# A chunked delta-rule stage on one core: right sides in turn with the last level's products, and GpSimd's streams behind VectorE's

## The reference

```python
def wkv_scan(r, w, k, v, kk, a, s0, reverse):
    def step(s, inp):
        r_t, w_t, k_t, v_t, kk_t, a_t = inp
        sa = jnp.einsum('bhij,bhj->bhi', s, -kk_t)
        s = (s * w_t[:, :, None, :] + sa[..., None] * (kk_t * a_t)[:, :, None, :]
             + v_t[..., None] * k_t[:, :, None, :])
        return s, jnp.einsum('bhij,bhj->bhi', s, r_t)
    ...

def rwkv_mix(streams, s0, ln_w, ln_b, r_k, g_up):
    r, v, kk, per_dir, gd = streams
    (wf, kf, af), (wb, kb, ab) = per_dir
    yf, sf = wkv_scan(r, wf, kf, v, kk, af, s0[0], False)
    yb, sb = wkv_scan(r, wb, kb, v, kk, ab, s0[1], True)
    y = yf + yb
    ...
    return y.reshape(b, l, D_RWKV) * g, (sf, sb)
```

## Time and profile before

| | us |
|---|---|
| median of 3 runs | 3325.36 |
| lowest and highest | 3323.35 and 3326.42 |
| the profiled execution's own time | 3319.18 |
| its span | 3317.4 |
| TensorE busy | 3078.1 (93%) |
| VectorE busy | 1578.4 (48%) |
| ScalarE busy | 564.4 (17%) |
| GpSimd busy | 1234.7 (37%) |

### The profile page before, as it was taken

How to read it: one execution, slowest core, us unless ns; L and a number is a source line. 1 busy time by engine, 2 the same in 40 slices (tenths; PEclk the granted TensorE clock), 3 DMA queues, 4 the chain that set the end, 5 groups by cost and what they waited for, 6 DMA issues and landing times.

```text
span 3317.4 us, 69293 instructions
## 1 busy us (share of the span) xinstructions
PE 3078.1 (93%) x32062; PEld 2768.7 (83%) x32062; DVE 1578.4 (48%) x2216; ACT 564.4 (17%) x1042; POOL 1234.7 (37%) x725
## 2 busy tenths in 40 slices
PE   4998998998999999999998788897999999999998
PEld 4877887877887888788698677777989999999998
DVE  4655276446337720378842677776344441113111
ACT  1022202011120120200002445453010000000001
POOL 2000010000000001134274454443648887777774
PEclk7998999998999999999999999999999999999999
DMA  7964288666226634367842000000546554444442
GB/s 269 420 242 181 103 315 317 269 263 241 104 100 241 259 126 183 127 249 297 310 160 91 6 6 9 6 6 26 193 151 233 222 208 169 162 178 147 162 176 101
DMA packets 55921, 583.08 MB, mean 176 GB/s; under 512 B 7202, under 2 KB 9568, under 8 KB 10704
## 3 DMA queue, kind: packets, MB, share of 16 engines
q1 hardware_dynamic: 38080, 466.11, 37.4%
q0 software_dynamic: 17552, 112.54, 8.9%
HBM read 576.52 MB, written 2.10 MB: 174 GB/s over the span
## 4 chain that ended last, share of the span: by engine, by line
PE 70%; DVE 14%; DMA 9%; issue 3%; POOL 2%; ACT 1%; SPq 0%; ACTq 0%; DVEq 0%; POOLq 0%
PE PS L1712 23%; PE PS L374 15%; PE PS L672 7%; PE PS L1665 5%; DMA ring<-in_w_vec_dram 4%; DMA ring<-in_w_second_dram 2%; PE PS L1891 2%; DVE ring L2304 2%; PE PS L417 2%; DMA ring<-in_w_start_dram 1%; PE PS L371 1%; PE PS L1908 1%; PE PS L1906 1%; PE PS L1837 1%; PE PS L1729 1%
## 5 line engine op out<-in xcount | busy, mean ns | idle before, releaser
L374 PE MATMUL PS<-H,ring 128*128 128x256 f32 x2944 | 668.8, 386 | 7.0 <-ACT H L702 7.0
L374 PEld LDWEIGHTS PS<-H,ring 128*128 128x128 f32 x2944 | 562.1, 193 | 94.9 <-issue 17.6
L1712 PE MATMUL PS<-H,ring 128*128 128x128 f32 x3424 | 403.9, 275 | 2.4 <-DMA ring<-in_w_second_dram 2.4
L1712 PEld LDWEIGHTS PS<-H,ring 128*128 128x128 f32 x3424 | 393.9, 192 | 3.2 <-DMA ring<-in_w_second_dram 2.8
L327 POOL DMA_DIRECT2D ring<-in_w_vec_dram x75 | 39.9, 532 | 930.3 <-DVE ring L888 790.5
L2411 DVE TENSOR_TENSOR W<-W,PS 128x256 f32<-128x256 f32 x58 | 24.4, 421 | 676.5 <-ACT W L2049 676.5
L1712 PE MATMUL PS<-H,W 128*128 128x128 f32 x2624 | 317.2, 277 | 10.9 <-POOL W L1541 9.2
L1712 PEld LDWEIGHTS PS<-H,W 128*128 128x128 f32 x2624 | 305.6, 193 | 12.5 <-POOL W L1541 9.9
L1536 POOL TENSOR_TENSOR W<-ring 128x1024 f32<-128x1024 f32 (+1 forms) x74 | 175.2, 2367 | 267.9 <-PE PS L1712 149.3
L672 PE MATMUL PS<-H,ring 128*128 128x256 f32 x1024 | 223.5, 379 | 2.9 <-DVE H L1174 2.9
L672 PEld LDWEIGHTS PS<-H,ring 128*128 128x128 f32 x1024 | 194.2, 190 | 29.9 <-issue 3.7
(11 more groups left out here) (496 smaller groups left out, 5015.5 us busy)
## 6 DMA issues: line engine op xcount, KB each, us to landing
ring<-in_w_second_dram SPq DMA_DIRECT2D x97, 2048.0 KB, 8.1
ring<-in_w_first_dram SPq DMA_DIRECT2D x68, 2048.0 KB, 8.2
ring<-in_w_vec_dram POOLq DMA_DIRECT2D x75, 1024.0 KB, 7.7
ring<-in_w_vec_dram SPq DMA_DIRECT2D x48, 1024.0 KB, 5.0
ring<-in_w_start_dram SPq DMA_DIRECT2D x16, 2048.0 KB, 15.7
H<-in_w_vec_dram POOLq DMA_DIRECT2D x21, 1024.0 KB, 7.9
Pj<-in_w_aside_dram SPq DMA_DIRECT2D x8, 2048.0 KB, 11.3
ring<-in_w_second_dram SPq DMA_DIRECT2D x9, 1536.0 KB, 6.5
```

The costliest lines, as they stand in the source:

```text
L374: mm = pe.matmul(PS[:, t % 2, half * T:(half + 1) * T], ring[:, t % 2, k, half * P:(half + 1) * P], hT[:, k, :], start=(k == 0), stop=(k = ...
L1712: mm = pe.matmul(regions(bank2, r), w[:, k * P:(k + 1) * P], m[:, k, :], start=(first and k == 0 and r // 4 not in opened), stop=(last and ...
```

## The change

It has these parts.

1. In level 5, TensorE issues the right sides' products (before: L1927, after the level) in turn with the level's own products, cell by cell. ScalarE's copy of them stands behind its copy of the level's products.
2. `turned_starts` stands ahead of level 1's first products, not between its two directions. The bank that it writes holds the backward scores, so it waits for a new semaphore, p_aTc.
3. The mask of level 1 is made by VectorE straight from the scores (into `mT`), not by GpSimd. The unmasked triangle is copied by ScalarE (p_aTc); `masks(j, 1)` goes from GpSimd.
4. GpSimd's `stream_back` for the pairs behind the first waits for p_streams (VectorE's last product), not for p_kk (its first).
5. VectorE's `sums` stand ahead of levels 4 and 5, not behind 4 and 5. On ScalarE the forward mixed keys and the spread stand ahead of the backward sigmoids.

```diff
@@ GpSimd
         def masks(j, lev):
             for d in range(2):
-                if lev == 1:
-                    need("p_aT", j, d + 1)
-                else:
-                    need("p_P", j, count(lev - 1, d))
+                need("p_P", j, count(lev - 1, d))
                 S("p_mask").inc(pool.tensor_tensor(mT[d], aT[d], each8(Ci(f"c_join{lev}")), ALU.mult))
...
             need("p_tm", j, 2)
-            need("p_kk", j, 1)
+            need("p_streams" if j else "p_kk", j, 1)
...
         for j in range(NP2):
-            masks(j, 1)
             masks(j, 2)
@@ TensorE
         def turned_starts(j):
-            need("p_xs", j, 2)
+            need("p_aTc", j, 2)
...
         def level(j, lev, between=None):
+            if lev == 1:
+                turned_starts(j)
             for d in range(2):
-                need("p_mask", j, count(lev, d))
                 if lev == 1:
-                    if d:
-                        turned_starts(j)
                     need("p_xs", j, d + 1)
                 else:
+                    need("p_mask", j, count(lev - 1, d))
                     need("p_xm", j, count(lev - 1, d))
                 for u in range(8):
+                    if lev == 5:
+                        for h in halves:
+                            bv = pe.matmul(PS[h, 2 + d, cell(u)], bT[d][h, u, :], VTok[d][h, u % 4, halves[u // 4]], start=True, stop=True)
                     for h, g in zip(halves, other):
                         mm = pe.matmul(PS[h, d, cell(u)], mT[d][g, u, :], xm[d][g, u, :], start=True, stop=True)
+                if lev == 5:
+                    done(bv, "p_bv")
                 done(mm, "p_P")
...
         def solved(j):
-            for d in range(2):
-                for u in range(8):
-                    hs = halves[u // 4]
-                    for h in halves:
-                        mm = pe.matmul(PS[h, 2 + d, cell(u)], bT[d][h, u, :], VTok[d][h, u % 4, hs], start=True, stop=True)
-                done(mm, "p_bv")
@@ ScalarE
             for d in range(2):
+                need("p_aT", j, d + 1)
+                f("p_aTc", aT[d].rearrange("p (r n) b -> p r (n b)", r=2), PS[:, 2 * d:2 * d + 2, 0:T], ACT.Copy)
                 need("p_BR", j, d + 1)
                 f("p_BRr", br[d], PS[:, 4 + 2 * d:6 + 2 * d, :].rearrange("p r (w c) -> p r w c", w=2), ACT.Copy)
...
                 f("p_Pc", pm[d], PS[:, d, :].rearrange("p (a b) -> p a b", b=CH), ACT.Copy)
+                if lev == 5:
+                    need("p_bv", j, d + 1)
+                    f("p_bvc", kbv[d][:, :, 64:P], PS[:, 2 + d, :].rearrange("p (u c) -> p u c", c=64), ACT.Copy)
...
             products(j, 4)
             if after:
+                key_mixes(j + 1, 0)
+                key_spread(j + 1)
                 sigmoids(j + 1, 1)
-                key_spread(j + 1)
             products(j, 5)
             if after:
-                key_mixes(j + 1)
+                key_mixes(j + 1, 1)
                 exponentials(j + 1, 0)
-            right_sides(j)
             solutions(j)
@@ VectorE
                 need("p_AX", j, d + 1)
-                o.do(v.tensor_tensor(per_head(aT[d]), heads(2 * d, 0), each(Ci("c_supper")), ALU.mult), S("p_aT"))
-                o.do(v.tensor_tensor(per_head(xm[d]), heads(2 * d, T), each(Ci("c_join0t")), ALU.mult))
+                o.do(v.tensor_tensor(per_head(mT[d]), heads(2 * d, 0), each(Ci("c_join1")), ALU.mult))
+                o.do(v.tensor_tensor(per_head(xm[d]), heads(2 * d, T), each(Ci("c_join0t")), ALU.mult), S("p_aT"))
...
+            if after:
+                sums(j + 1, 0)
             level(j, 4)
             if before:
                 normed(j - 1)
             if after:
-                sums(j + 1, 0)
+                sums(j + 1, 1)
...
             level(j, 5)
             if after:
-                sums(j + 1, 1)
                 keys(j + 1)
```

More of the change, by code:

```diff
@@ L2169, in key_spread, with key_mixes @@
             f("p_kbig", kbig.rearrange("p (a b) -> p a b", b=CH), knorm.unsqueeze(2).to_broadcast([P, 8, CH]), ACT.Copy)
-        def key_mixes(j):
+        def key_mixes(j, d):
             need("p_kssq", j, 1)
-            need("p_sig", j, 4)
-            for d in range(2):
-                f("p_tm", TMP[d], AA[d], ACT.Identity, scale=col(j, U_KA), bias=sm[:, j + 80:j + 81])
+            need("p_sig", j, 2 * d + 2)
+            f("p_tm", TMP[d], AA[d], ACT.Identity, scale=col(j, U_KA), bias=sm[:, j + 80:j + 81])
         def exponentials(j, d):
@@ L2233, in pairs_act @@
         key_spread(0)
-        key_mixes(0)
+        for d in range(2):
+            key_mixes(0, d)
         for d in range(2):
```

9 lines of the change are left out of this document (2 added, 7 removed).

## The result

| | before | changed | changed, measured once more |
|---|---|---|---|
| median (runs), us | 3325.89 (4) | 3305.86 (4) | 3297.80 (5) |
| lowest and highest, us | 3323.35, 3328.74 | 3302.67, 3307.30 | 3293.46, 3303.61 |
| ratio to before, 95% interval | | 0.9940 (0.9926 to 0.9955) | 0.9918 (0.9902 to 0.9934) |
| profiled execution: span, us | 3317.4 | 3300.9 | 3291.7 |

The change is faster by 20 us (26 us in the second measurement, each against runs of before made beside it). The forecast was 3305.5. The total is right. Of its terms some are not, and the experiments show that the parts don't add up as the forecast added them.

A forecast was written before the change was run, and what follows sets the result against it. TensorE, busy 93% of the span, was taken to bound the kernel. 2.6 + 0.2 = 2.8 us a pair over seven pairs, plus 0.2 in the last, gave 3325.4 - 19.8 = 3305.6, told as 3305.5; range 3295 to near 3320.

The forecast's parts named there:

- Level 5 and the right sides: Level 5's products and the right sides' products, issued in turn, take 2.2 us: minus 1.9, and ScalarE's copy 0.4 earlier.
- Rival A, the supply of instructions: Dense mixed products outrun instruction supply, new or longer stops near L1934; gain falls to about 1.6 a pair, 3314; chance 0.17.
- It is wrong if new issue stops stand around L1934: Sign against the forecast: new TensorE stops marked issue around L1934, or L1837 waiting by more than 1 us.
- The stop of 0.95: TensorE's issue stop at 2067.27 in the fourth pair, kept in the forecast; under rival A it might grow to 1.5 and more.
- What is late next: Chains to the state steps: TensorE 2.9 us earlier, VectorE's stream shorter, GpSimd last by 0.3; gain 2.6 us a pair.
- The lock on the forward sum: VectorE's forward sum waits for GpSimd's masks; level 4's subtractions 1.9 us late, reaching nobody at level 5; 0.4 a pair.
- The start of a pair: L1877 ends 0.6 earlier, VectorE's last two instructions gain 0.2 us a pair, between 0 and 1.2.
- The sum: 2.6 + 0.2 = 2.8 us a pair for seven pairs, 19.6; the last pair counts only its start, 0.2.
- Rival B: GpSimd's stream, now behind VectorE's, is last by far: L1837 starts 1.1 to 1.5 us later, 3336; chance 0.07.

## Why the prediction was right, and where it was not

- **Level 5 and the right sides.** Right. 2.0 us for the mixed products (2050.65 to 2052.6) against 2.2 forecast, and TensorE's busy time 1.8 to 2.3 less a pair with all parts. L1929 comes 2056.91 - 2025.44 = 31.5 behind L2543 in place of 32.8; 30.9 was forecast. The missing 0.6 is less than the stop of 0.97 that stands there now.
- **Rival A, the supply of instructions, given 0.17.** Partly true, and the sharpest part of the forecast's own list: "It is wrong if new issue stops stand around L1934". One stands ahead of it, in L1909 or the keys' norm, in each of the first seven pairs of one profile (0.17 to 1.00 us, 5.1 in all) and in four of the other (2.5 in all); before there was none. The stop of 0.95 was 1.20 in one profile and 0.93 in the other, so it did not grow for certain. The size is not A's: all stops grew by 7.4 us over the way in one profile and 1.4 in the other, not seven times 1.2. The Trainium skill, Runtime: NRT & Kernel Launch, section Instruction fetch mechanics, has instructions come in blocks of 256, which the fixed count of records bears out. "Mostly hidden" is true of most of the 14 crossings of a pair and false of the five or so in its dense phases, which cost up to 1.6 us each on the two ways.
- **What is late next.** Half right. VectorE's products 0.68, 0.29 and 0.69 as forecast (0.7, 0.4, 0.7), GpSimd's stream behind them, 2061.86 to 2070.07: 8.2 us, forecast 8.0. But the end is set by TensorE, not by GpSimd: L1967 starts 40.6 behind L2543, where it was 42.0 and 39.1 was forecast, so 1.4 gained and not 2.9, and the third L1833 does not wait. TensorE's stops (0.97, 1.20) are most of the difference, and they hide GpSimd's bound, which ended at 2070.07, 0.2 ahead of the third L1833. With VectorE's sums late the bound shows, 5.3 us.
- **The lock on the forward sum.** Right, and right that it reaches nobody at level 5. The price of 0.4 us a pair (the difference of 3305.5 and 3302.7) does not show: level 5's subtractions ran at 2054.92 and 2055.93, and the keys' product waited 0.40 for its norm at 2057.01. That was the place where the delay was to show. By the Trainium skill, SBUF — State Buffer, section Who interferes with whom, the sum was to be locked; the trace agrees (2.16 against 1.22), and the time doesn't care.
- **The start of a pair.** Too small: 0.2 us forecast, 0.7 a pair less to wait for VectorE, and 5 to 13 us in the ratios. The value taken was near the lower end of its 0 to 1.2, and the clock was put at nothing: nowhere does the prediction look at it, though the trace of before has it at 0.50 behind the wait of 2.0 us in four of the seven pairs.
- **The sum.** 2.8 a pair; the two profiles give 2.0 and 3.2. It came out because an under-sized start and an over-sized middle lie on both sides, not because each term held. That the total is right is luck in this part.
- **Additivity.** The step that failed in kind: the forecast added parts, and costed part 4 as a few tenths of a bound. The runs show a condition. Mixing without it is 29 us slower, all parts without it 5 us slower than before, and it alone is worth nothing. The early sums are of use only with mixing. Rival B had the two streams' lock as the mechanism of a loss, but only for the changed kernel, where the order prevents it.

What stays open: how much of the gain is ScalarE's new order (a part of 5 that no run undid alone), and whether mixing is worth 4 or 11 us in the full change. Parts 2 to 4 with ScalarE's order (0.9954) against part 4 alone (1.0001) leave about 15 us to the start and ScalarE's order together. By the run without it the start is 5 to 13 us, but in another company, and the parts here do not add.

## What to carry to other kernels

When two edits meet at one place, ask what the second is worth without the first: here getting TensorE on earlier took away a pause that had kept two other engines apart, and that turned 2 us a pair gained into 4 us a pair lost, until an ordering wait kept the two apart for good. Price a wait of TensorE, a new one or one that goes, with the clock behind it as well as its own length. Where dense small products go by, count the records from the program's start: stops come at fixed counts, so an inserted or removed instruction far ahead moves them, and a difference of up to 10 us between two such kernels says nothing about the edit.

## What the runs showed of the hardware that was not expected

- Copies are held up as products are: VectorE's copy of 128x8 took 1.22 us beside GpSimd's stream, 0.17 without; the one of 128x256 1.25 and 0.29. The sum's scan took 2.16 beside masks, 1.22 without.
- The same eight instructions of VectorE took 4.0, 6.5, 7.6 or 9.1 us, in all seven pairs of a kernel alike, by how long GpSimd's eight stayed beside them.
- The stops lie on a lattice of 252 to 256 records of TensorE, fixed to within two records over four lengths of the program and two executions of one. Each ends 1.2 to 1.7 us behind the landing of a 16 KB packet of the instruction queue. Their length varies (0.70 and 0.97, 0.93 and 1.20), and whether one is seen at all.
- Behind waits of 1.4 to 5.8 us for VectorE in the steps the granted clock was 0.50, in all seven pairs of both kernels that had them, and in the kernel without part 4 that cost 13.3 us of busy time beside 17.1 us of waiting. Behind a wait of 2.0 us at the start of a pair it was 0.50 in four pairs of seven before.
- A product of two columns with 128x128 f32 weights is not cheap: 64 of them took about 22 us.
